# Splitting the plain products around the layer starts, and moving a few Vector and Scalar instructions, in a two-block fp32 transformer kernel

## The reference

```
for l in range(2):
    h = rmsnorm(x, norm_mix[l]);  p = h @ w_in[l] + b_in[l]       # 1024 -> 6144
    merged = sigmoid(p_s) * mlstm(p_m, p_z) + sigmoid(p_t) * conv31(p_a, p_g)
    x = x + merged @ w_out[l]
    x = x + cross_attention(rmsnorm(x, norm_x[l]), rmsnorm(mem, norm_mem[l]), wq, wk, wv, wo)
    x = x + conv_ffn(rmsnorm(x, norm_ffn[l]), ...)                # 1024 -> 2 x 2816 -> 1024
```

## Time and profile before

| | before |
|---|---|
| median of 3 runs | 2650.57 us (2647.05 to 2650.60) |
| the profiled execution | 2649.37 us, its span 2647.5 us |
| TensorE busy | 2587.2 us, 98% of the span |
| VectorE busy | 2189.2 us, 83% |
| ScalarE busy | 1540.3 us, 58% |
| read from memory | 663.72 MB, 252 GB/s over the span |

### The profile page before, as it was taken

One profiled execution on the slowest core, in us unless ns is written; L12 is line 12 of the kernel. 1 busy time (PEld: TensorE's weight loads), 2 busy tenths in 40 slices (PEclk: granted clock), 3 DMA queues, 4 the chain that ended last, 5 costly groups with the idle time before them and its releaser, 6 DMA issues.

```text
span 2647.5 us, 37681 instructions
## 1 busy us (share of the span) xinstructions
PE 2587.2 (98%) x15563; PEld 2303.3 (87%) x15563; DVE 2189.2 (83%) x2485; ACT 1540.3 (58%) x1626; POOL 49.8 (2%) x84
## 2 busy tenths in 40 slices
PE   7999999999999999999999999999999999999998
PEld 6889988887888888888888799998899999998998
DVE  6988877798989899999989889975477799864877
ACT  3534345576777777777777755544454566344554
POOL 1010000000000000000000000000000000000000
PEclk9999999999999999999999999999999999999999
DMA  9669964399999999999999854443555534554453
GB/s 325 224 245 371 351 212 158 128 385 334 359 377 354 357 361 374 352 358 369 357 353 366 320 171 148 150 172 129 184 196 182 179 127 136 165 191 153 161 184 111
DMA packets 376496, 670.44 MB, mean 253 GB/s; under 512 B 27129, under 2 KB 199935, under 8 KB 371455
## 3 DMA queue, kind: packets, MB, share of 16 engines
q1 hardware_dynamic: 358336, 662.02, 70.8%
q10 hardware_dynamic: 17983, 5.94, 0.9%
HBM read 663.72 MB, written 4.19 MB: 252 GB/s over the span
## 4 chain that ended last, share of the span: by engine, by line
PE 88%; DVE 6%; ACT 3%; issue 2%; DMA 1%; POOL 0%; ACTq 0%; DVEq 0%; POOLq 0%; SPq 0%
PE PS L459 25%; PE PS L461 25%; PE PS L460 25%; DVE LO L454 2%; PE PS L2818 2%; PE PS L567 2%; PE PS L1745 2%; ACT HI L435 1%; PE PS L775 1%; DMA AR<-in_w_ada_dram 1%; PE PS L2857 1%; PE PS L2711 1%; PE PS L2702 1%; PE PS L2874 1%; DMA RAW<-in_w_ada_dram 0%
## 5 line engine op out<-in xcount | busy, mean ns | idle before, releaser
L454 DVE TENSOR_TENSOR LO<-RAW,HI 128x2048 fp32r<-128x2048 f32 x409 | 927.4, 2273 | 158.7 <-ACT HI L435 156.1
L435 ACT ACTIVATE HI<-RAW 128x2048 fp32r<-128x2048 f32 x410 | 780.7, 1905 | 334.0 <-PE PS L461 296.8
L459 PE MATMUL PS<-X1H,HI 128*128 128x256 f32 (+1 forms) x2128 | 608.7, 286 | 13.2 <-DVE X1L L649 7.3
L460 PE MATMUL PS<-X1L,HI 128*128 128x256 f32 (+1 forms) x2128 | 604.6, 284 | 0.0
L461 PE MATMUL PS<-X1H,LO 128*128 128x256 f32 (+1 forms) x2128 | 604.5, 284 | 0.0
L459 PE MATMUL PS<-HI,X1H 128*128 128x512 f32 x1056 | 420.2, 398 | 5.9 <-DVE LO L454 4.6
L459 PEld LDWEIGHTS PS<-X1H,HI 128*128 128x128 f32 (+1 forms) x2128 | 408.3, 192 | 18.8 <-issue 16.4
L461 PE MATMUL PS<-HI,X1L 128*128 128x512 f32 x1056 | 412.9, 391 | 0.0
L460 PE MATMUL PS<-LO,X1H 128*128 128x512 f32 x1056 | 412.5, 391 | 0.0
L460 PEld LDWEIGHTS PS<-X1L,HI 128*128 128x128 f32 (+1 forms) x2128 | 408.6, 192 | 1.8
L461 PEld LDWEIGHTS PS<-X1H,LO 128*128 128x128 f32 (+1 forms) x2128 | 408.5, 192 | 0.8
(11 more groups left out here) (419 smaller groups left out, 2813.3 us busy)
## 6 DMA issues: line engine op xcount, KB each, us to landing
RAW<-in_w_in_dram SPq DMA_DIRECT2D x66, 1024.0 KB, 5.4
RAW<-in_expert_w_down_dram SPq DMA_DIRECT2D x66, 1024.0 KB, 7.1
RAW<-in_expert_w_gate_dram SPq DMA_DIRECT2D x64, 1024.0 KB, 7.3
RAW<-in_expert_w_up_dram SPq DMA_DIRECT2D x62, 1024.0 KB, 7.0
RAW<-in_ffn_w_up_dram SPq DMA_DIRECT2D x55, 1024.0 KB, 5.6
AR<-in_expert_w_up_dram SPq DMA_DIRECT2D x50, 1024.0 KB, 7.0
AR<-in_expert_w_gate_dram SPq DMA_DIRECT2D x48, 1024.0 KB, 6.9
AR<-in_expert_w_down_dram SPq DMA_DIRECT2D x46, 1024.0 KB, 7.2
```

Of the source, the lines that this page charges most:

```text
L435: a.activation(HI[:, n % NH, 0:size(i)], raw_at(i), ACT.Copy).then_inc(*hi.up(i))
L454: v.tensor_tensor(LO[:, m % NH, 0:n], raw_at(i), HI[:, m % NH, 0:n].bitcast(F32), ALU.subtract).then_inc(*lo.up(i))
L459: t.matmul(o, lh, rh, start=first, stop=False)
L460: t.matmul(o, lh, rl, start=False, stop=False)
```

## The change

Five edits are made together.

1. The plain product that stands ahead of the transposes is cut: 12 of its 16 products stay ahead, 4 come behind. This is done for `ek` 2 (n1 of layer 0), `ek` 4 (n1 of layer 1), `ek` 3 (nf of layer 0) and the third value unit (nx of both layers). The last value unit is cut in three: 4 products ahead of the scores, 10 behind them, 2 between the first and the second pair of turned heads.
2. On ScalarE the copy-out of the early keys (`act_early`) moves behind `act_fm_scaled`, and the copy-out of the last values moves between the second and the third turned head.
3. At the start of the second block, `act_squares` moves ahead of one `split_hi`.
4. In the experts' first steps the places are made in step 1 (was 3), the first high and low rows in step 2 (was 3), and the second bias is added in step 4 (was 5).
5. The ring of slots is turned at four units, so that some units swap slots.

```diff
+    TURNS = {moe_first + 7: (4,), moe_first + 14: (3, 5), moe_first + 21: (2, 4), moe_first + 28: (3,)}
     for i in range(len(plan)):
+        for p in TURNS.get(i, ()):
+            ring[p], ring[p + 1] = ring[p + 1], ring[p]
...
-    def pe_keys(t, i, cols, bank):
+    def pe_keys_begun(t, i, cols, bank, n):
 
         t.wait_ge(*raw[slot_of[i]](i))
         pe_key_part(t, i, cols, bank, 0, range(8))
-        pe_key_part(t, i, cols, bank, 1, range(8)).then_inc(*used.up(i))
+        return pe_key_part(t, i, cols, bank, 1, range(n))
+
+    def pe_keys_ended(t, i, cols, bank, n):
+        pe_key_part(t, i, cols, bank, 1, range(n, 8)).then_inc(*used.up(i))
...
     def act_between(a, x, b, after):
-        if x + 1 in FIRSTS and (b, after) == (3, "u"):
+        if (x, b, after) == (0, 2, "u") or x in (2, 4) and (b, after) == (3, "u"):
             act_high_rows(a, x + 1, 0)
...
-        if x + 1 in FIRSTS and (b, after) == (3, "u"):
+        if (x, b, after) == (0, 1, "u") or x in (2, 4) and (b, after) == (3, "u"):
             dve_places(v, x + 1)
+        if (x, b, after) == (0, 2, "u") or x in (2, 4) and (b, after) == (3, "u"):
             dve_low_rows(v, x + 1, 0)
...
-                if n in (3, 5):
-                    dve_scaled_bias(v, n // 2 - 1)
+                if n in (3, 4):
+                    dve_scaled_bias(v, n - 3)
...
-        pe_keys(t, CH["ek"][2], raw_cols(CH["mf"][1]), 2)
+        pe_keys_begun(t, CH["ek"][2], raw_cols(CH["mf"][1]), 2, 4)
...
-            pe_keys(t, CH["ek"][4], MF, 2)
+            pe_keys_begun(t, CH["ek"][4], MF, 2, 4)
         pe_to_fm(t, ("n1", l), XN, [4, 5, 6, 7], lambda nb: dve_two("normed", nb, "mix", l))
+        pe_keys_ended(t, CH["ek"][4 if l else 2], MF if l else raw_cols(CH["mf"][1]), 2, 4)
...
-        rows_of_values(2, 2)
+        rows_of_values(2, 2, 0, 12)
 
         pe_to_fm(t, ("nx", l), XN, [4, 5, 6, 7], lambda nb: dve_two("normed", nb, "x", l))
+        rows_of_values(2, 2, 12, 16)
...
+        t.wait_ge(*act_ev(f"xq{l}", 2))
+        rows_of_values(3, 0, 0, 4)
         t.wait_ge(*act_ev(f"xq{l}", 3))
...
-        rows_of_values(3, 0)
+        rows_of_values(3, 0, 4, 14)
         for h in range(4):
             b = 2 + h % 2
             t.wait_ge(*dve_two("xp", h, l))
+            if h == 0:
+                t.wait_ge(*act_ev(f"xv{l}", 2))
+            if h == 2:
+                rows_of_values(3, 0, 14, 16)
...
-            pe_keys(t, CH["ek"][3], MF, 2)
+            pe_keys_begun(t, CH["ek"][3], MF, 2, 4)
...
+        if l == 0:
+            pe_keys_ended(t, CH["ek"][3], MF, 2, 4)
...
         if l == 0:
             act_early(a, 1, 4)
             act_early_out(a, 1)
+        act_squares(a, X, xn, lambda q: dve_two("ffnx", q, 0) if l else dve_res("x", 1, 1, q), "mix", l)
+        if l == 0:
             split_hi(a)
-        act_squares(a, X, xn, lambda q: dve_two("ffnx", q, 0) if l else dve_res("x", 1, 1, q), "mix", l)
+        act_fm_scaled(a, ("n1", l), [4, 5, 6, 7], X1H, lambda c: pcol(f"norm_mix{l}", c))
         n = 4 if l else 2
         act_early(a, n, 2)
         act_early_out(a, n)
-        act_fm_scaled(a, ("n1", l), [4, 5, 6, 7], X1H, lambda c: pcol(f"norm_mix{l}", c))
...
-        ev_values(3, 0)
         for h in range(4):
+            if h == 2:
+                ev_values(3, 0)
```

More of the change, by code:

```diff
@@ L1747, in pe_key_part, with pe_keys @@
         return z
-    def pe_keys(t, i, cols, bank):
+    def pe_keys_begun(t, i, cols, bank, n):
         t.wait_ge(*raw[slot_of[i]](i))
         pe_key_part(t, i, cols, bank, 0, range(8))
-        pe_key_part(t, i, cols, bank, 1, range(8)).then_inc(*used.up(i))
+        return pe_key_part(t, i, cols, bank, 1, range(n))
+    def pe_keys_ended(t, i, cols, bank, n):
+        pe_key_part(t, i, cols, bank, 1, range(n, 8)).then_inc(*used.up(i))
+    def pe_keys(t, i, cols, bank):
+        pe_keys_begun(t, i, cols, bank, 8).then_inc(*used.up(i))
     EARLY_ROOM = [ar(o, 512) for o in (16128, 11528, 12040, 11528, 12040)]
@@ L2809, in keys, with rows_of_values @@
             pe_keys(t, CH[f"xk{l}"][j], MF, b)
-        def rows_of_values(j, b):
+        def rows_of_values(j, b, n0=0, n1=16):
             i = CH[f"xv{l}"][j]
-            t.wait_ge(*raw[slot_of[i]](i))
+            if n0 == 0:
+                t.wait_ge(*raw[slot_of[i]](i))
             w = raw_at(i).rearrange("p (c n) -> p c n", c=8)
[L2816 to L2820, removed]
+            for n in range(n0, n1):
+                k, c = n // 8, n % 8
+                z = t.matmul(PS[:, b, 256 * k:256 * k + 256], MF[:, c, 128 * k:128 * k + 128], w[:, c, :],
+                             start=(c == 0), stop=(c == 7))
+            if n1 == 16:
+                z.then_inc(*used.up(i))
         t.wait_ge(*act_two("memory", l))
@@ L2868, in pe_layer2 @@
                      for n_ in range(2) for k in range(2)]).then_inc(*pe_two.up("xpt", h, l))
+        t.wait_ge(*act_ev(f"xv{l}", 3))
         for h in range(4):
             t.wait_ge(*act_two("xpt", h, l))
-            t.wait_ge(*act_ev(f"xv{l}", h))
             for dc in range(2):
@@ L2885, in pe_layer2, with done @@
         pe_to_fm(t, ("nf", l), XN, [4, 5, 6, 7], lambda nb: dve_two("normed", nb, "ffn", l))
+        if l == 0:
+            pe_keys_ended(t, CH["ek"][3], MF, 2, 4)
         key = f"ff2{l}"
+        def done(n, p):
+            if n == 0 and l == 0:
+                t.wait_ge(*act_ev("ek", 3))
         pe_ffn(t, key, ("nf", l), lambda p: act_ffn(key, "pad", p, 0), lambda p: act_ffn(key, "pad", p, 1),
-               lambda n, p: None, lambda: None)
+               done, lambda: None)
     def xn(k, ns):
@@ L3083, in act_layer2 @@
         act_squares(a, X, xn, lambda q: dve_two("attx", q, l), "ffn", l)
+        act_fm_scaled(a, ("nf", l), [4, 5, 6, 7], X1H, lambda c: pcol(f"norm_ffn{l}", c))
         if l == 0:
@@ L3086, in act_layer2 @@
             act_early_out(a, 3)
-        act_fm_scaled(a, ("nf", l), [4, 5, 6, 7], X1H, lambda c: pcol(f"norm_ffn{l}", c))
         split_hi(a)
```

## The result

| | before | after |
|---|---|---|
| median, these runs | 2649.38 us (2647.05 to 2650.60) | 2634.09 us (2632.52 to 2635.76) |
| the profiled execution | 2649.37, span 2647.5 | 2635.76, span 2634.0 |
| TensorE busy | 2587.2 | 2582.4 |
| read from memory | 663.72 MB | 663.72 MB |

The ratio is 0.9945, with an interval of 0.9932 to 0.9958: about 14.6 us faster; the two medians lie 15.3 apart and the two profiled executions 13.6. The prediction said 8.4 us and 2642.2, with 2637.5 as its lower end. It took 8.4 off a median of three, 2650.57; with a fourth run of the kernel before, the median is 2649.38, so 1.2 us of the miss is in this base.

What follows compares the result with a forecast made beforehand. TensorE is busy 98% of the span, so only its waits, some 60 us, can be won. Terms -1.6 - 0.9 - 1.4 - 1.2 - 1.2 - 2.1 = -8.4 us, from 2650.57 to 2642.2; own range 2639.5 to 2644.5, with rivals 2637.5 to 2647.5.

Steps and rivals of the forecast that it cites:

- So the earlier loads gain 0 as well.: Key products of `ek` 1 and 2 follow the scatter without a wait, so loading them earlier was priced at 0.
- rival on the ring: Experts: transfers issued one unit later land after their splits and hold TensorE; slower, 2657 us; chance 0.03.
- The clock stays at 1.00 ... So the moved products win their own wait and no more.: Start of layer 0, second block: no slow-clock stretch seen, so nothing added for a gain of a few us.
- Start of layer 0, -0.9: Second block: first unit begins at 1541.4 instead of 1542.11 (0.7), plus 0.2 from no longer being paced by VectorE.
- Each filled wait, by its own length: TensorE's waits filled with moved products were priced at the length of the wait, without more.
- nx, nf, scores and shares: Filled waits: -1.2 for both nx starts, -1.2 at nf of layer 0, -2.1 for scores and shares of two layers.
- more than worked out: Rival: waits shorter than the overlap of two products' ends go too; -13 us, 2637.5; chance 0.08.
- steps 3 and 5: Experts' first steps: TensorE's waits of 1.11 and 1.95 us vanish, a gain of 3.06 before the moved work's cost.
- the new waits in steps 1 and 2: Experts: the moved places cost 0.87 in step 1, the moved low rows 0.6 in step 2.
- no wait in step 4: Experts: the moved bias, 1.22, costs 0 beside TensorE's small products, with 0.3 as the other end.
- the copy-out as part of the 1.19: Feed-forward of layer 0: early keys' copy-out belongs to the 1.19 us wait; moving it readies the low parts in time.
- no cost of the late third unit: Layer 0, second block: the unit lands at about 1547.0, is ready at 1551.4 and needed at 1553.0; cost 0.

## Why the prediction fell short

- **"So the earlier loads gain 0 as well."** This is the step that failed, and the largest. The prediction asked only whether the data of `ek` 1 and 2 would be missed, and found no wait for them. What the turned ring does is to issue their loads at 1497.23 and 1500.43 instead of 1508.77 and 1512.55, so that both have landed when TensorE comes to its branch. All six profiles with the second load on its way there have idle times of 3.7 to 3.9 us; all eight others have 1.4 to 1.6. Alone it gives 4.9 us in the profile and 3.0 in the medians; taking it out of the changed kernel costs 2.3 and 2.8. The prediction's rival on the ring looked the other way, to late transfers. The 3.9 us stood in the list of waits as "issue", and the prediction did not name it.
- **"The clock stays at 1.00 ... So the moved products win their own wait and no more."** The row that was weighed covers one start. At two other places of the same profile the clock was at 0.50, behind 3.88 and 1.95 us of idle time; no row of these was looked at. Over all fourteen profiles: behind 3.7 to 3.9 us the slow stretch came each time, behind 2.2 in two of three, behind 1.95 in two of six, behind 1.05 or less at this start never; but behind the 1.14 us at 487 it came in seven of fourteen, where only transposes and products of 64 columns stand ahead of the wait. The Trainium skill (TensorE: Matmul & The Clock Gate, "Why this matters for your kernels") warns of idle gaps above about 3 us. The rows of the scatter agree, and those of 2.2, 1.95 and 1.14 us show that shorter ones can cost the clock too.
- **Start of layer 0, -0.9.** Wrong in its sign as soon as the ring is turned. TensorE gets to the end of its products earlier, X does not, and the four products moved behind the transposes only lengthen the idle time ahead of them: 2.23 us, where 1.0 was predicted. Left whole they are worth 0.8 (19.28 against 20.07), 2.4 with the slow stretch. The squares gave 0.58 instead of 1.8: they wait for X. So the start is 0.2 longer than with the ring alone (20.07 against 19.86), and 1.9 with the slow stretch. With the old ring the term held in the main: the transposes wait 0.91 where 1.0 was predicted, and the two edits give 22.27 - 20.78 = 1.5, of which some part is clock.
- **Each filled wait, by its own length.** The mechanism was right at nx, nf, scores and shares; the terms were 0.1 to 0.5 too small at each place. A filled wait also gives back the overlap of the products on its two sides. The rival "more than worked out" named this, and it is 2.3 us here: 0.9 at scores and shares, 0.5 at nx, 0.2 at nf, 0.1 at n1 of layer 1, 0.5 in steps 3 and 5.
- **Right:** the new waits in steps 1 and 2 (0.87 and 0.6 against 0.79 and 0.58), no wait in step 4, no cost of the turned ring inside the experts, the copy-out as part of the 1.19, and no cost of the late third unit in the changed kernel (it landed at 1542.2, the products behind it go on without a gap). This last one is luck in part: the start of layer 0 was itself late. Where TensorE is earlier against that load, in the kernel without the ring and in the one with four products in the idle time, it waits for `LO` at the fourth unit and loses 0.9 and 0.6. The prediction had this as "with 1 us more on the load it would cost 0.6".

In sum: the prediction's -8.4, then -2.1 net at the scatter and the start of layer 0, -1.6 for a slow stretch that the profile of before happened to have, -2.3 for overlap and -0.1 in steps 1 and 2: -14.5. This sum is for the two profiled executions. Two of its parts, the 1.6 behind step 5 and the slow stretch behind the 2.23 us, vary from one execution to the next, as does the 1.6 at 487 outside it, so it does not explain the medians to better than a few us.

**What stays open.** The instruction packet starts late where the 1 MB load was issued ahead of the branch and had not landed; that it stands behind this load in the DMA engines' queues fits all six profiles, but no run moved the load by itself in small steps. The trace does not say which engine the packet serves: it always comes between TensorE's branch and its first product. How often the slow stretches come is known only from single profiles, and that the idle time in front brings them was tried once, with four products in it, in one profile.

## What to carry to other kernels

An idle time that the trace calls "issue" at a branch is not fixed: look up when the branch instruction starts, and if a large load was issued shortly ahead of it and has not landed, hold back or pull forward that load. Fill a wait only where TensorE is the one that is late; where the input comes from another engine's chain, moving products behind it makes the gap in front longer. Extra work for VectorE belongs ahead of splits that have idle time in front, not behind the product that TensorE is about to need.

## What was not expected of the hardware

A branch costs TensorE 1.4 to 1.6 us of idle time, and 3.7 to 3.9 when a load of 1 MB was issued 0.95 us ahead of it: the instruction packet behind the branch then starts 3.5 to 3.7 us after it instead of 1.1 to 1.4. The same idle time, 2.2 us at the same place, was followed by a granted clock of 0.50 in two executions and of 1.00 in another. A wait of 1.95 us that is filled gives 2.2, one of 0.63 gives 0.98 at nx.
